# A seven-for-eight block at the head of the first down trip: a hybrid decoder layer on one Trainium2 core

## The reference

```python
h = rmsnorm(x, norm_ffn_g[l])
x = x + jnp.square(jax.nn.relu(h @ w_up[l])) @ w_down[l]      # w_up 2048x8192, w_down 8192x2048
return rmsnorm(x, final_g)
```

## Time and profile before

| | |
|---|---|
| time, median of 3 runs | 1507.49 us |
| the profiled execution's own time | 1507.86 us |
| its span | 1506.1 us |
| PE busy | 1493.8 us, 99% |
| DVE busy | 1248.7 us, 83% |
| ACT busy | 778.6 us, 52% |
| share of the 16 DMA engines | 61.1% |
| granted TensorE clock, mean | 0.999 of full speed |

### The profile page before, as it was taken

The page is one execution under the profiler, slowest core; times in us unless marked ns, Lnnn a source line. Parts: engine busy times, 40 slices in busy tenths (PEclk is TensorE's granted clock), DMA queues, the critical chain, the costliest instruction groups (busy, mean ns, idle before and its releaser), DMA issues.

```text
span 1506.1 us, 21236 instructions
## 1 busy us (share of the span) xinstructions
PE 1493.8 (99%) x7618; PEld 1263.8 (84%) x7618; DVE 1248.7 (83%) x1669; ACT 778.6 (52%) x974; POOL 2.0 (0%) x11
## 2 busy tenths in 40 slices
PE   8999999999999999999999999999999999999998
PEld 7888888888888888888888888888888888888886
DVE  6668889988889879988976779987898779987897
ACT  5544444465554456556565455545554545544554
POOL 0000000000000000000000000000000000000000
PEclk9999999999999999999999999999999999999999
DMA  9666665655556666665655656655666566656662
GB/s 301 192 182 191 189 195 179 211 180 178 176 179 197 192 198 196 209 205 188 196 182 180 194 183 210 209 186 177 209 197 207 169 202 205 195 179 209 210 203 89
DMA packets 209980, 291.12 MB, mean 193 GB/s; under 512 B 9227, under 2 KB 129107, under 8 KB 209778
## 3 DMA queue, kind: packets, MB, share of 16 engines
q1 hardware_dynamic: 209906, 290.14, 61.1%
HBM read 287.48 MB, written 2.10 MB: 192 GB/s over the span
## 4 chain that ended last, share of the span: by engine, by line
PE 99%; DMA 0%; ACT 0%; SPq 0%; DVE 0%; issue 0%
PE acc L1491 27%; PE acc L1510 14%; PE acc L1511 14%; PE acc L1512 14%; PE acc L1489 13%; PE acc L1561 3%; PE acc L1560 3%; PE acc L1559 3%; PE acc L1484 2%; PE acc L1587 1%; PE acc L1486 1%; DMA y_tok<-in_x 0%; PE acc L1639 0%; PE acc L1660 0%; PE acc L1529 0%; PE acc L1531 0%
## 5 line engine op out<-in xcount | busy, mean ns | idle before, releaser
L579 ACT ACTIVATE w_hi<-w_raw 128x1024 fp32r<-128x1024 f32 x502 | 524.4, 1057 | 441.5 <-PE acc L1512 237.5
L846 DVE TENSOR_TENSOR w_lo<-w_raw,w_hi 128x1024 fp32r<-128x1024 f32 x502 | 605.4, 1221 | 139.8 <-ACT w_hi L579 135.8
L1491 PE MATMUL acc<-h_hl,w_hi 128*128 128x512 f32 x1740 | 546.7, 395 | 0.0
L1489 PEld LDWEIGHTS acc<-h_hl,w_lo 128*128 128x128 f32 x1740 | 322.3, 188 | 72.4 <-issue 0.6
L1489 PE MATMUL acc<-h_hl,w_lo 128*128 128x256 f32 x1740 | 343.6, 279 | 0.0
L1491 PEld LDWEIGHTS acc<-h_hl,w_hi 128*128 128x128 f32 x1740 | 265.2, 189 | 0.0
L1510 PE MATMUL acc<-w_hi,m_hl 128*128 128x512 f32 x424 | 165.3, 390 | 0.0
L1512 PE MATMUL acc<-w_hi,m_hl 128*128 128x512 f32 x424 | 165.0, 389 | 0.0
L1511 PE MATMUL acc<-w_lo,m_hl 128*128 128x512 f32 x424 | 165.0, 389 | 0.0
L1510 PE MATMUL acc<-w_hi,h_hl 128*128 128x512 f32 x336 | 132.2, 394 | 0.0
L1512 PE MATMUL acc<-w_hi,h_hl 128*128 128x512 f32 x336 | 130.8, 389 | 0.0
(11 more groups left out here) (270 smaller groups left out, 1654.7 us busy)
## 6 DMA issues: line engine op xcount, KB each, us to landing
w_raw<-in_w_in SPq DMA_DIRECT2D x200, 512.0 KB, 4.4
w_raw<-in_w_up SPq DMA_DIRECT2D x128, 512.0 KB, 4.3
w_raw<-in_w_down SPq DMA_DIRECT2D x128, 512.0 KB, 4.5
w_raw<-in_w_mix_out SPq DMA_DIRECT2D x32, 512.0 KB, 4.0
w_raw<-in_w_sconv_out SPq DMA_DIRECT2D x16, 512.0 KB, 3.8
w_raw<-in_w_attn_out SPq DMA_DIRECT2D x16, 512.0 KB, 4.3
w_raw<-in_w_conf_out SPq DMA_DIRECT2D x16, 512.0 KB, 3.8
bias_row<-in_gate_b SPq DMA_DIRECT2D x10, 256.0 KB, 4.3
```

What stands on the lines that cost most here:

```text
L579: act.activation(w_hi[:, q], w_raw[:, raw], ACT.Copy).then_inc(hi_done, 1)
L846: dve.tensor_tensor(w_lo[:, q], w_raw[:, raw], w_hi[:, q].bitcast(F32), ALU.subtract).then_inc(lo_done, 1)
L1489: pe.matmul(*narrow[m], start=False, stop=False)
L1491: last = pe.matmul(*wide[m], start=False, stop=final)
```

## The change

The first down trip of each chunk (t == 0) gets a fourth quad, at step 0. Its slabs are (0, 1) and (1, 1), since the sums `a_forms` exist only for odd i (the first set was stored and unused); (0, 0) and (1, 0) follow as plain slabs. Its sums of weights are formed and split in steps 4 to 7 of the chunk's last up trip, by the same functions: `quad_at` maps a step beyond the end of the last up trip to the down trip's first steps. The last up trip is therefore written out instead of run as an iteration of the loop. In that quad PE takes the products in another order: it first waits for both slabs and all the sums, and begins with the products of sums, in banks that the up phase does not use.

```diff
 PAIR = [(0, 0), (0, 1), (1, 0), (1, 1), (0, 2), (1, 2), ...]
+EARLY = [(0, 1), (1, 1), (0, 0), (1, 0)]
...
+    if ph.name == "down" and t == 0:
+        return [(n, i, KDOWN) for n, i in EARLY + PAIR[4:] + PAIR_ENDS[False]]
...
+    if t == 0:
+        return (0, 6, 10, 14)
     return (6,) if last_trip(ph, c, t) else (6, 10, 14)
+
+def quad_at(ph, c, t, k):
+    if k >= ph.nslabs and ph.name == "up" and isinstance(t, int) and t == ph.trips - 1:
+        ph, t, k = PH["down"], 0, k - ph.nslabs
+    return (ph, c, t, k) if k in quads(ph, c, t) else None
...
         body(PH["up"], c, 0)
-        loop("up", c, first=1)
+        loop("up", c, first=1, last=1)
+        body(PH["up"], c, PH["up"].trips - 1)
...
-                    if k + 3 in quads(ph, c, t):
-                        forms_second(ph, c, t, k + 3)
+                    if quad_at(ph, c, t, k + 3):
+                        forms_second(*quad_at(ph, c, t, k + 3))
...                                     # the same for forms_first, forms_lo, forms_hi, hi and lo
+                    if 0 in quads(ph, c, t):
+                        first = first and (n, m) == (1, 1)
...
+                if k == 0:
+                    pe.wait_ge(lo_done, s + 2)
+                    pe.wait_ge(t_lo, quad * 2 + 2)
+                    pe.wait_ge(f_lo, c * 4 + (stored + 1 + AHEAD_FORMS))
+                    pe.wait_ge(p_sum, pair_of(ph, c, t) * P_SUMS)
+                    product(P_BANK["P6"], form(S2), summed(T2), True, False)
+                    product(P_BANK["P7"], form(S3), summed(T3), True, False)
+                    product(P_BANK["P5"], form(S1), summed(T1), True, False)
+                    product(P_BANK["P1"], whole(0, 2 * i), loaded(w_x, 0), True, False)
+                    pe.wait_ge(evac_done, group_of(ph, c, t, 0) - 1)
+                    product(4, whole(0, 2 * i + 1), loaded(w_x, 1), True, False).then_inc(slab_used, 1)
+                    product(5, whole(1, 2 * i + 1), summed(T4), True, False)
+                    pe.wait_ge(evac_done, group_of(ph, c, t, 1) - 1)
+                    product(6, form(S4), loaded(w_y, 1), True, False).then_inc(slab_used, 1)
+                    return
```

More of the change, by code:

```diff
@@ L148, in quad_of @@
         return t * 3 + at
-    return GATE_QUADS + at if ph.name == "mix" else c * (3 * PH["down"].trips) + t * 3 + (at + GATE_QUADS + MIX_QUADS)
+    return GATE_QUADS + at if ph.name == "mix" else c * 7 + t * 4 + (at + GATE_QUADS + MIX_QUADS)
 def pair_of(ph, c, t):
@@ L167, in trip_behind @@
         return ph, c, t - 1
-    if ph.name == "up" and isinstance(t, int) and not (isinstance(c, int) and c == 0):
+    if ph.name == "up" and isinstance(t, int) and t == 0 and not (isinstance(c, int) and c == 0):
         return PH["down"], c - 1, PH["down"].trips - 1
@@ L201, in walk, with loop @@
 def walk(eng, body):
-    def loop(name, c=0, first=0):
-        with eng.Fori(first, PH[name].trips) as t:
+    def loop(name, c=0, first=0, last=0):
+        with eng.Fori(first, PH[name].trips - last) as t:
             body(PH[name], c, t)
@@ L575, in hi @@
                 q = ahead % RING
-                if ahead - 1 in quads(ph, c, t):
+                if quad_at(ph, c, t, ahead - 1):
                     act.activation(half_rows(w_hi[:, q], 1), half_rows(w_raw[:, raw], 1), ACT.Copy).then_inc(hi_done, 1)
@@ L581, in forms_hi @@
             def forms_hi(ph, c, t, k):
-                if k + 2 in quads(ph, c, t):
-                    act.wait_ge(t_raw, quad_of(ph, c, t, k + 2) * 2 + 2)
+                if quad_at(ph, c, t, k + 2):
+                    act.wait_ge(t_raw, quad_of(*quad_at(ph, c, t, k + 2)) * 2 + 2)
                     act.activation(forms_of(ph)[:, 0, 2:4, :], w_sums[:, 2:4, :], ACT.Copy).then_inc(t_hi, 1)
-                if k + 1 in quads(ph, c, t):
+                if quad_at(ph, c, t, k + 1):
                     act.activation(forms_of(ph)[:, 0, 0:2, :], w_sums[:, 0:2, :], ACT.Copy).then_inc(t_hi, 1)
@@ L841, in lo @@
                 dve.wait_ge(hi_done, s + (LOOKAHEAD + 1))
-                if k + LOOKAHEAD - 1 in quads(ph, c, t):
+                if quad_at(ph, c, t, k + LOOKAHEAD - 1):
                     dve.tensor_tensor(half_rows(w_lo[:, q], 1), half_rows(w_raw[:, raw], 1),
@@ L1263, in trip @@
                         token_sums(*trip_behind(ph, c, t))
[L1264 to L1269, removed]
+                    if quad_at(ph, c, t, k + 4):
+                        forms_first(*quad_at(ph, c, t, k + 4))
+                    if quad_at(ph, c, t, k + 2):
+                        forms_lo(*quad_at(ph, c, t, k + 2), 0)
+                    if quad_at(ph, c, t, k + 1):
+                        forms_lo(*quad_at(ph, c, t, k + 1), 1)
                     n, i, size = order_of(ph, c, t)[k]
```

## The result

The changed kernel takes 1521.72 us, the median of four executions (1520.53 to 1525.61), against 1507.35 us before, also of four: ratio 1.0099, 95% interval 1.0087 to 1.0111. The sign and the main mechanism are as forecast, the size is not: + 14.4 us in place of + 8.6, and 1521.72 lies above the range's 1520.5. Its profiled execution took 1521.02 us with a span of 1519.2.

What follows compares the result with a forecast made beforehand. PE, busy 99% of the span, was taken to bound the kernel. Per chunk + 2.84 - 0.68 = + 2.16 us, for four + 8.6, from 1507.86 to 1516.5, less 0.37 for the median: 1516.1 us; range 1512.8 to 1520.5.

Steps and rivals of the forecast that it cites:

- sign: Whole kernel: the change makes it slower, by 0.57%; slower by more than 0.2% was given 0.93.
- main mechanism: New block at the down phase's start: PE idles until DVE's second split of sums is done, outweighing the matmuls saved.
- what the block saves: First down trip of each chunk: 21 matmuls replace 24, saving 0.68 us a chunk, 2.72 us for four.
- the gap: Ahead of each chunk's new block: PE idles 2.84 us waiting for DVE's last split of sums.
- no second wait behind the first: Down phase after the gap: slab 3's split is done at 1078.4, wanted at 1079.8, 1.4 us to spare.
- The written-out trip instead of a loop iteration costs nothing: Last up trip of each chunk: writing it out adds no time, since PE crosses the loop ends shown without a gap.
- rival 1, the clock: In the gap PE's clock falls to its lower level, costing 1.6 us a chunk: 1522.5 us; chance 10%.
- 2.7 is shorter than 3.2: Argument against a clock fall: PE's 2.7 us idle is shorter than the 3.2 us before the fall at kernel end.
- Rival 2: Down phase: slab 3's or ACT's spare time is used up, a second wait costs about 1 us a chunk: 1520; 8%.
- Rival 3: New block: DVE's sums are in time, PE has no gap, 1504.8 us, 0.18% faster; chance 5%.
- Rival 4: New block: a chunk keeps its 24 matmuls, so the kernel is slower by the gap alone, 1518.8 us; chance 1%.

Runs made afterwards that it cites:

- e3: Changed kernel with the loop over the two middle chunks written out, the new block as it is: 1517.48 us, ratio 1.0071.
- e7: On e2, the down trip's fourth-slab split made ahead of the squared ReLU, that group's a_forms formed at down step 7: 1504.94 us, ratio 0.9983.
- filled kernel: Changed kernel with twelve matmuls of unused result at the head of each new block, ahead of its wait for the sums: 1515.77 us, ratio 1.0054.
- Experiments 1 and 2: Changed kernel with the new block's products reordered (e1), 1514.47 us; that with the middle chunks' loop written out (e2), 1509.23 us; the writing-out alone (e3), 1517.48 us.
- e5: Kernel before with only the last up trip of each chunk written out, no new block: 1512.66 us, ratio 1.0034.
- e10: e5 plus twelve matmuls of unused result in the first chunk, ahead of the loop over the middle chunks: 1510.36 us.
- e8: Changed kernel with twelve matmuls of unused result in the first chunk alone, ahead of the middle chunks' loop: 1518.03 us.
- after_again: The changed kernel, unaltered, measured once more beside later runs on the same chip: 1524.03 us (1519.62 to 1528.02), ratio 1.0106.
- e9: Changed kernel with twelve matmuls of unused result in the middle chunks alone, inside their loop: 1523.62 us.
- e11: Changed kernel with sixty matmuls of unused result in the first chunk alone, ahead of the middle chunks' loop: 1528.12 us.
- e1: Changed kernel with the new block's products reordered by when operands are ready, each waiting only for what it reads: 1514.47 us, ratio 1.0046.
- e6: The filled kernel: changed kernel with twelve matmuls of unused result at the head of each new block, in all chunks: 1515.77 us, ratio 1.0054.
- e2: e1 with the loop over the two middle chunks written out: 1509.23 us, ratio 1.0011.

## Why the prediction was wrong

**Right: what the block saves and the gap.** I forecast - 0.68 and + 2.84 us a chunk. Measured are - 0.59 and + 2.73: the first two matmuls behind the gap are 0.33 apart instead of 0.227 (0.31 in e3), which takes 0.08 to 0.10 of the saving, and DVE's end of the last split (1073.81) stands 0.24 us before PE's start, where I had taken 0.15; the other 0.2 is that DVE was through with that split earlier relative to PE. The stand is not the only thing that takes from the saving: e7 has no gap, and its chunks save only 0.54 to 0.60, with three distances of 0.24 to 0.26 in its second down phase; why they are longer stays open. The sum of the two, + 8.6, is + 8.50 in the profile. The filled kernel, which has neither stops nor falls, is at 1515.77 us, where I forecast 1516.1.

**Right: no second wait behind the first.** DVE starts the fourth slab's split at 1078.64 and ends it at 1079.87; at the full clock PE would want it at 1074.05 + 33 x 0.2268 = 1081.5, so 1.7 us were to spare (forecast: 1.4), and PE went on without a gap. Experiments 1 and 2 show that this rested on the first gap.

**Wrong: "The written-out trip instead of a loop iteration costs nothing: PE crosses all loop ends of rows 2 without a gap".** This step failed. The stretch of rows 2 ends at 1152.00, and before branches back over the middle chunks at 1152.46, so it does not hold the branch back. (Before has no gap there either: from 1150 to 1320 PE is busy all 170.00 us.) And that the old code comes in time says nothing of a loop over the middle chunks that is 261 instructions longer on PE and begins 250 later. It cost 3.3 us in the profile, and 5 us where it was isolated (e5 against e10), since the clock can fall in the stops as well. The runs showed in its place that PE stops at the branch back and fetches its code again where the loop begins 9016 or 9022 instructions in, and not where it begins at 9040 or later. The instruction transfers of before (none in the second pass) were a row to read first.

**Wrong in size: rival 1, the clock.** I took the fall as one case for all chunks and gave it 10%, with 1.6 us a chunk. One fall costs 1.4 to 1.65 us, about as I said (once 2.9, e9), but it comes in some gaps and not in others: one in the profile, two in the repeated one, none in the profile of e3, in all 5 of the 20 gaps of 2.5 to 2.7 us in the profiles of after, after_again, e3, e8, e9 and e11. In the stops it came in 3 of 5 profiles (after_again, e5, e9; not in after and e1). So it is no rival but a term of the sum. Without any fall the changed kernel would take 1507.4 + 8.5 + 3.3 = 1519.2 us, and its nine executions lie 0.4 to 8.8 us above that. It was the argument "2.7 is shorter than 3.2" that failed: the gap of 2.57 us is enough at times.

With stops of 3.3 and one fall or two the sum is 1507.4 + 8.5 + 3.3 + 1.65 to 3.3 = 1520.9 to 1522.5, around the measured 1521.72. Either term alone (stops 1519.2, falls 1517.5 to 1519.2) would have left the time inside the range; together they take it out.

**Rivals 2, 3, 4** did not occur: the down phases have no second wait, the gap is 2.69 to 2.73 us in every chunk, and PE does 12 matmuls less.

## What to carry to other kernels

A saving of matmuls is worth its count only if each operand is still ready one matmul sooner: before moving operand work ahead, list the deadlines of the next few operands too, since hiding the first wait (e1) calls up the next. Order the products of a block by when their operands are ready (e1), and the splits of a vector engine by when they are needed, not by where they are written (e7). A loop on TensorE that is long in instructions (about 1600 here) is timed by its place in the program as well: after every edit look for instruction transfers and for stops at the branch, and write such a loop out if it has them (e3). A TensorE that has to stand for some 2.7 us anyway does better with unused matmuls (e6).

## What was not expected of the hardware

- Idle times of 2.5 to 2.7 us let the clock fall to the lower level in some cases and not in others of the same length. In the profile after it fell 1.2 us after work had begun again (from 1075.32 the matmuls are 0.43 us apart, and behind 1079 at full clock again), in the repeated one while PE still stood; 1.4 to 1.65 us are lost each time, once 2.9. With gaps of 0.9 us (e2) 11 executions lie within 0.7 us.
- 24 instructions more ahead of a loop, without a change in it, were worth 3.3 us (the stops of after, gone in e8) to 5.0 (e5 against e10).
- Why a loop begun 9016 or 9022 instructions in has the stops and one begun at 9040 or later has not, stays open.
